# Layer norm, modulation, Hyena filters, long convolutions and the first head pair's projections written as one program block

## The reference, cut to what matters

```python
mod = (c @ w_ada + b_ada)[:, None, :]
shift, scale, gate = jnp.split(mod, 3, axis=-1)
h = (_layer_norm(x) * (1.0 + scale) + shift).astype(x.dtype)
p = h @ w_in + b_in
p_qkv, g_attn, p_hy, g_hy, r_merge = jnp.split(p, [i1, i2, i3, i4], axis=-1)
...
u = centred_conv3(p_hy, conv_w, conv_b)
v, x1, x2 = jnp.split(u, 3, axis=-1)
filters = implicit_filters(S, filt_w1, ...)     # 3 sine layers of width 64, then @ filt_w4, times a decay
z = v
for o, gate_o in enumerate((x1, x2)):
    z = gate_o * (bidirectional_long_conv(z, filters[:, o, 0], filters[:, o, 1]) + filt_bias[o] * z)
y_hy = z * jax.nn.silu(g_hy)
```

## Time and profile before

| what | value |
|---|---|
| median of 3 runs | 2665.92 us (2662.88 to 2666.19) |
| the profiled execution's own time | 2664.33 us |
| its span, first to last instruction | 2662.5 us |
| PE busy | 2415.2 us, 91% |
| DVE busy | 1003.7 us, 38% |
| ACT busy | 592.3 us, 22% |
| POOL busy | 243.0 us, 9% |
| mean granted PE clock | 0.937 |

### The profile page before, as it was taken

How to read it: one execution, slowest core, us unless ns; L and a number is a source line. 1 busy time by engine, 2 the same in 40 slices (tenths; PEclk the granted TensorE clock), 3 DMA queues, 4 the chain that set the end, 5 groups by cost and what they waited for, 6 DMA issues and landing times. The chain is left out here.

```text
span 2662.5 us, 23256 instructions
## 1 busy us (share of the span) xinstructions
PE 2415.2 (91%) x9479; PEld 1601.8 (60%) x9479; DVE 1003.7 (38%) x1690; ACT 592.3 (22%) x1010; POOL 243.0 (9%) x156
## 2 busy tenths in 40 slices
PE   6889998999958999999999999989598898998998
PEld 2433443444326777676776778866374675557975
DVE  3264441542442022322223222357766322344255
ACT  0210101001013233232332333101121343322032
POOL 0000000000002111111111112211000110000000
PEclk9788999999988999898998999999799899999999
DMA  7301022211203111111110121130410112003000
GB/s 278 96 27 44 20 83 77 78 51 59 63 24 103 48 33 32 39 34 32 37 36 25 41 83 44 44 140 31 138 16 4 40 40 91 1 1 127 36 36 40
DMA packets 131232, 151.18 MB, mean 57 GB/s; under 512 B 14501, under 2 KB 106115, under 8 KB 130309
## 3 DMA queue, kind: packets, MB, share of 16 engines
q1 hardware_dynamic: 119734, 107.82, 12.7%
q0 software_dynamic: 11392, 41.87, 4.7%
HBM read 136.89 MB, written 11.60 MB: 56 GB/s over the span
## 5 line engine op out<-in xcount | busy, mean ns | idle before, releaser
L168 PE MATMUL banks<-h_hi,da_w_rest 128*128 128x512 f32 x896 | 364.1, 406 | 40.5 <-DVE h_rest L1334 40.5
L169 PE MATMUL banks<-h_rest,da_w_hi 128*128 128x512 f32 x896 | 354.3, 395 | 0.0
L170 PE MATMUL banks<-h_hi,da_w_hi 128*128 128x512 f32 x896 | 353.0, 394 | 0.0
L434 PE MATMUL banks<-arena 128*128 128x512 f32 x512 | 242.0, 635 | 12.9 <-DMA arena<-in_w_in 12.9
L168 PEld LDWEIGHTS banks<-h_hi,da_w_rest 128*128 128x128 f32 x896 | 171.3, 191 | 96.8 <-issue 59.1
L584 PE MATMUL banks<-arena 128*128 128x512 f32 x480 | 209.9, 598 | 7.8 <-DMA arena<-in_fwd_C 3.7
L1005 POOL TENSOR_TENSOR da_w_rest<-arena,da_w_hi 128x1024 fp32r<-128x1024 f32 x56 | 134.5, 2402 | 712.2 <-ACT da_w_hi L1168 712.2
L434 PEld LDWEIGHTS banks<-arena 128*128 128x128 f32 x512 | 103.7, 205 | 154.8 <-issue 145.8
L1328 DVE COPY arena<-banks 128x768 f32<-128x768 f32 (+1 forms) x64 | 52.8, 825 | 378.9 <-PE banks L1081 378.9
L170 PEld LDWEIGHTS banks<-h_hi,da_w_hi 128*128 128x128 f32 x896 | 170.9, 191 | 37.6
L169 PEld LDWEIGHTS banks<-h_rest,da_w_hi 128*128 128x128 f32 x896 | 171.7, 192 | 33.3
(11 more groups left out here) (353 smaller groups left out, 3694.9 us busy)
## 6 DMA issues: line engine op xcount, KB each, us to landing
arena<-in_w_in SPq DMA_DIRECT2D x80, 512.0 KB, 3.8
arena<-in_w_ada POOLq DMA_DIRECT2D x6, 2048.0 KB, 10.5
arena<-in_decay SPq DMA_DIRECT2D x32, 256.0 KB, 2.9
arena<-in_x SPq DMA_DIRECT2D x4, 1024.0 KB, 15.2
arena<-in_fwd_P POOLq DMA_DIRECT2D x4, 1024.0 KB, 6.8
arena<-in_fwd_M POOLq DMA_DIRECT2D x4, 1024.0 KB, 8.3
arena<-in_fwd_B POOLq DMA_DIRECT2D x4, 1024.0 KB, 5.6
arena<-in_w_out SPq DMA_DIRECT2D x8, 512.0 KB, 7.6
```

The lines of the kernel that those rows point to most:

```text
L168: nc.tensor.matmul(out, ll, rh, start=start, stop=False)
L169: nc.tensor.matmul(out, lh, rl, start=False, stop=False)
L170: return nc.tensor.matmul(out, lh, rh, start=False, stop=stop)
L434: last = nc.tensor.matmul(PS[:, 2 * (n % 2) + h, :], self.wt[:, n % 4, k, :], self.hT[:, k, h * 512:(h + 1) * 512], start=(k == 0), stop=( ...
```

## The change

`prepare`, `hyena` and the start of `dilated_attention` become one block, `front`, with one hand-written order for each engine.

- The filter network works on both directions at once: 128 partitions by 1024 columns in place of 64 by 2048, so 6 products in place of 12. Filter rows take the two directions as two 64-row products side by side (partitions 0 to 63 and 64 to 127). The decay is computed by ACT as an exponential, no longer loaded. Filters come before the modulation; the spectra of order 1 are made first, written to DRAM and read back for order 1.
- Chunks 0 to 3 of the modulation use `c` itself as the stationary operand, one column wide (L441 of the changed kernel), and give one row; the two chunks of `gate` stay 128 columns wide.
- The transform has eight leaves of 128 complex points (N, C, B0, B1, P0, M0, P1, M1), 4 products each, in place of the five leaves with 60. An inverse takes 4 products a leaf as well. The leaves come out of DVE in three steps (`cyclic`, `cyclic_b`, `negacyclic_leaves`), and PE may start on a leaf once its step is done.
- The 16 Hyena projections are split products as well, in one stream of 26 tiles (`T_ALL`) with the 10 of head pair 0, over one weight ring. Leaves and inverses stand between tiles 4 and 5, 7 and 8, 11 and 12, and behind 12. The convolution adds its outer taps straight from PSUM.
- `dilated_attention` begins with the value rows; its first weights, tiles 10 and 11, and the distance table are loaded there.

The diff, cut to its core:

```diff
+            def filter_rows(stage, t):
...
+                bank_free(g, t)
+                for d in range(2):
+                    last = nc.tensor.matmul(PS[:, 4 + 2 * (t % 2) + d, :], h3[HD * d:HD * d + HD, t * P:(t + 1) * P], w4[HD * d:HD * d + HD, a, :],
+                                            start=True, stop=True)
+                last.then_inc(f_mm, 1)
...
+            def modulation(i):
...
+                for k in range(KT):
+                    if i < 2:
+                        last = nc.tensor.matmul(PS[:, 2 + i % 2, :], cbc[:, k, :], wada[:, i % 2, k, :], start=(k == 0), stop=(k == KT - 1))
+                    else:
+                        last = nc.tensor.matmul(PS[0:1, 2 + i % 2, :], cols2[:, 39 + k:40 + k], wada[:, i % 2, k, :], start=(k == 0), stop=(k == KT - 1))
+                last.then_inc(mod_done, 1)
...
+            def forward(g, l, base, first, ready, mm, loads):
+                done = groups[g][1]
+                pe.wait_ge(mat_in[l], 16 * loads)
+                pe.wait_ge(ready, done // 8 * 3 + LEAF_STEP[l])
+                bank_free(g, l)
+                ins = leaf_inputs(l, base, first)
+                for part in range(2):
+                    for k in range(2):
+                        last = nc.tensor.matmul(PS[:, 4 + 2 * (l % 2) + part, :], mats[:, l, k * 256 + part * P:k * 256 + part * P + P], ins[k],
+                                                start=(k == 0), stop=(k == 1))
+                last.then_inc(mm, 1)
...
+            def project(T):
+                pe.wait_ge(w_rest, T + 1)
+                if T >= 2:
+                    if T - 2 < X2:
+                        pe.wait_ge(row_ready, T - 1)
+                    elif T - 2 < GHY:
+                        pe.wait_ge(conv_done, T - 1)
+                    else:
+                        pe.wait_ge(p_ready, T - 1)
+                for h in range(2):
+                    for k in range(KT):
+                        if T == 0 and k % 2 == 0:
+                            pe.wait_ge(h_rest[h], k // 2 + 1)
+                        if h == 1 and k == 4 and 1 <= T <= X2:
+                            to_rows(T - 1)
+                        last = split_product(nc, PS[:, 2 * (T % 2) + h, :], tuple(v[:, k * P:(k + 1) * P] for v in w_parts[T % 2]),
+                                             tuple(v[:, k % 2, h * 512:(h + 1) * 512] for v in K.h_parts[k // 2]), k == 0, k == KT - 1)
+                    last.then_inc(proj_mm, 1)
+
...
+            for layer in range(3):
+                network(layer)
+            for t in range(NT):
+                filter_rows(0, t)
+            for i in range(3):
+                modulation(i)
+            for l in range(4):
+                forward(1, l, 3, 5, hl_ready, hs_mm, 1)
+            modulation(3)
+            for l in range(4, 8):
+                forward(1, l, 3, 5, hl_ready, hs_mm, 1)
+            modulation(4)
+            modulation(5)
...
+            for T in range(5):
+                project(T)
+            for l in range(8):
+                forward(3, l, 3, 5, hl_ready, hs_mm, 1)
+            for T in range(5, X2):
+                project(T)
+            for l in range(8):
+                forward(4, l, 6, 3, zl_ready, zs_mm, 1)
+            for l in range(8):
+                inverse(0, l)
+            for T in range(X2, GHY):
+                project(T)
+            for l in range(8):
+                forward(6, l, 6, 3, zl_ready, zs_mm, 3)
+            project(GHY)
+            for l in range(8):
+                inverse(1, l)
+            for T in range(GHY + 1, T_ALL):
+                project(T)
...
+            act.wait_ge(filt_in, 16 * 8)
+            decays(0, 0)
+            decays(0, 1)
+            act.wait_ge(nmr_ready, 1)
+            for t in range(2, NT):
+                decays(0, t)
+                normalise(t - 2)
...
+            def multiply(a, l):
...
+                dve.wait_ge(zs_mm, 8 * a + l + 1)
+                if a == 0 and l == 0:
+                    dve.wait_ge(hs_ready, 16)
+                if a == 1 and l % 4 == 0:
+                    dve.wait_ge(h1_in, 32)
+                nc.vector.tensor_tensor(t01, PS[:, b:b + 2, :], H, ALU.mult)
+                nc.vector.tensor_tensor(t23[:, 0, :], PS[:, b, :], hi, ALU.mult)
+                link(nc.vector.tensor_tensor(t23[:, 1, :], PS[:, b + 1, :], hr, ALU.mult), taken)
...
+                    link(nc.vector.tensor_tensor(hi, t23[:, 0, :], t23[:, 1, :], ALU.add))
+                    link(nc.vector.tensor_tensor(hr, t01[:, 0, :], t01[:, 1, :], ALU.subtract), products)
...
+            fold_filter(0)
...
+            total_and_difference(tile(4, 0, 4), tile(4, 4, 4))
+            cyclic(h_leaves)
+            cyclic_b(h_leaves)
+            negacyclic(3)
+            negacyclic_leaves(3, 5, h_leaves)
...
+            fold_filter(1)
...
+                nc.vector.tensor_tensor(lo[:, :, 0:512], hT[:, 2 * c:2 * c + 2, 0:512], hi[:, :, 0:512].bitcast(fp32), ALU.subtract).then_inc(h_rest[0], 1)
+            total_and_difference(tile(4, 0, 4), tile(4, 4, 4))
+            cyclic(h_leaves)
+            convolve(0)
+            cyclic_b(h_leaves)
+            negacyclic(3)
+            convolve(1)
+            negacyclic_leaves(3, 5, h_leaves)
+            for T in range(2, 5):
+                convolve(T)
+            dve.wait_ge(row_ready, 4)
+            dve.wait_ge(hs_mm, 16)
+            split_rows()
+            cyclic(z_leaves)
+            convolve(5)
+            cyclic_b(z_leaves)
+            negacyclic(6)
+            convolve(6)
+            negacyclic_leaves(6, 3, z_leaves)
+            convolve(7)
+            for l in range(8):
+                multiply(0, l)
+            recombine_cyclic(0)
+            convolve(8)
+            recombine_negacyclic(0)
+            convolve(9)
+            dve.wait_ge(row_ready, 8)
+            link(nc.vector.tensor_tensor(tile(6, 0, 8), tile(6, 0, 8), tile(5, 0, 8), ALU.mult), Count(z1_ready))
+            split_rows()
+            cyclic(z_leaves)
+            convolve(10)
+            cyclic_b(z_leaves)
+            negacyclic(6)
+            convolve(11)
+            negacyclic_leaves(6, 3, z_leaves)
+            for l in range(8):
+                multiply(1, l)
+            recombine_cyclic(1)
+            recombine_negacyclic(1)
...
-            for n in range(halves):
-                project(n)
...
-            round_weights(0)
-            for h in range(2):
-                for c in range(4):
-                    half = slice(h * 512, (h + 1) * 512)
-                    nc.scalar.copy(K.h_parts[c][0][:, :, half], hT[:, 2 * c:2 * c + 2, half]).then_inc(h_hi, 1)
-                if h == 0:
-                    round_weights(1)
-            act.wait_ge(yhy_out, 16)
-            for n in range(halves):
-                take_projection(n)
+            round_weights(TILES)
+            round_weights(TILES + 1)
+            act.wait_ge(K.yhy_out, 16)
```

More of the change, by code:

```diff
@@ L261, in _, with decays @@
         @block.scalar
         def _(act):
-            act.wait_ge(var_ready, 1)
-            nc.scalar.activation(std, mv[:, :, 1], ACT.Sqrt).then_inc(std_ready, 1)
+            def decays(stage, t):
+                n = 8 * stage + t
+                if n >= 2:
+                    act.wait_ge(f_ready, n - 1)
+                for d in range(2):
+                    last = nc.scalar.activation(dec[:, t % 2, d, :], delta, ACT.Exp, scale=tcol[:, 8 * d + t:8 * d + t + 1])
+                last.then_inc(dec_ready, 1)
@@ new lines, in _ @@
+            for layer in range(3):
+                act.wait_ge(fn_arg, layer + 1)
+                nc.scalar.activation(h3 if layer == 2 else hA, hA, ACT.Sin).then_inc(fn_sin, 1)
+            act.wait_ge(var, 1)
+            nc.scalar.activation(rstd, mv[:, :, 1], ACT.Sqrt).then_inc(std, 1)
+            act.wait_ge(filt_in, 16 * 8)
[5 more added lines that the diff above has]
+                normalise(t - 2)
@@ new lines, in negacyclic_leaves @@
+            def negacyclic_leaves(v, first, signal):
+                x0, x1, y0 = two((v, 0), (v, 2)), two((v, 4), (v, 6)), two((v, 1), (v, 7))
+                for x, l0, cy0, cy1 in ((x0, 0, C8, -S8), (x1, 2, S8, C8)):
+                    axpy(both(first, l0), y0, cy0, x)
+                    axpy(tile(first, l0), tile(v, 5), cy1, tile(first, l0))
+                    axpy(tile(first, l0 + 1), tile(v, 3), cy1, tile(first, l0 + 1))
+                    axpy(x, x, 2.0, both(first, l0), ALU.subtract, signal if l0 else None)
@@ L290, in _ @@
+            statistics(0)
+            statistics(1)
+            network(1)
+            for i in range(2, 6):
+                statistics(i)
+            network(2)
+            statistics(6)
+            statistics(7)
             for i in range(NT):
                 link(nc.vector.bn_aggr(mv[:, i, :], stats[:, i, :]))
-            link(nc.vector.tensor_scalar(mv[:, :, 1], mv[:, :, 1], 1e-5, None, ALU.add), Count(var_ready))
```

(7 more changed lines are left out.)

1067 lines of the change are left out of this document (504 added, 563 removed).

## The result

The changed kernel takes 2434.19 us (median of 4 runs, 2432.76 to 2436.55), the kernel before beside it 2666.06 us: ratio 0.913, 95% interval 0.912 to 0.915. That is 231.9 us less. The forecast was 2417, so it was 17 us too low: 1 us above the forecast's own range (2402 to 2433) and inside the whole range (2400 to 2460).

The account below looks back on a forecast made before the run. The first 922 us were taken as bound by PE, with holes at the start and of 39 us. Gain 251 less 3 for hand-overs, 248, from 2664.3 gives 2416; with 1.6 to the median, 2417; range 2400 to 2460.

Parts of the forecast that it names:

- (a): Start of the front block: 26 small loads put the first PE instruction at 16 us, bounds 9.7 and 24.
- (b): Filter network: three layers take 36.5 us, to 52.5; aggregation and ACT's table loads follow, to 60.3.
- (d): PE-bound modulation chunks 41.2 us, eight leaves 27.4, one-column products 4.6, clock ramp 2, wait 1.6: ends at 151.
- (e): Filling hT until 173 us, then PE waits for DVE's fold, 9.6, and first piece of h_rest, 1.7: 184.4.
- (g): DVE starts the spectrum products at 312 us, 4.1 a leaf; the inverse runs behind and ends at 369.
- (h): Tiles 8 to 11: convolution 8 ahead of recombine_negacyclic, convolution 9 at 407.7 us; PE waits 5, to 418.6.
- (i): DVE's gate, split, leaf steps and convolutions from 407.7 to 444.5 us; PE idles some 20; last leaf ends at 472.
- (k): Tiles 13 to 25 take 141.7 us, to 652.5; each needs its weights within 10.9.
- (l): End of front: eviction and barrier 2.7 us, distance table issue 2, landing 11.3, scaling 2; first value copy at 671.
- rival 1: Modulation: the clock falls in the four one-column chunks, +28 us, 2445; chance 27%.
- Rival 2: DVE comes too late for the transposes if PSUM or strided-pair passes are 15% longer: +45 us, 2462; chance 15%.
- The sum of 189 us: PE work saved in the front: projections 45 us, forward products 96, inverses 43, filter network 5.

Follow-up runs that it names:

- the fold behind the split: Changed kernel with the second filter's fold on VectorE behind the four subtractions of h instead of ahead of them: 2432.73 us.
- the five moves: Changed kernel with table early, convolution 8 behind recombination, tile 12 in the hole, h's rest on VectorE ahead of the fold, convolution 0 right behind it: 2402.60 us.
- two rests sooner: Against the kernel that makes weight rests of tiles 0 to 12 on VectorE, not GpSimd: those of tiles 2 and 3 moved forward; 2389.38 us.

## Why the prediction was right, and where not

The walk against the traces, in us; the last column is the run in which GpSimd only fills:

| point | walk | changed kernel | with the fill |
|---|---|---|---|
| first PE instruction (a) | 16 | 14.1 | 14.8 |
| first filter row (b) | 60.3 | 56.2 | - |
| transposes into hT begin (d) | 151 | 152.0 | - |
| tile 0 begins (e) | 184.4 | 188.4 | 188.2 |
| spectrum products begin (g) | 312 | 332.2 | 320.9 |
| convolution 9 ends (h) | 407.7 | 432.0 | 414.5 |
| third leaf's product begins on DVE (i) | 444.5 | 471.2 | 451.7 |
| last tile ends (k) | 652.5 | 677.5 | 658.6 |
| first value copy (l) | 671 | 691.3 | 672.6 |

In row (i) the walk's figure is the end of DVE's leaf step and the trace's the first product behind it.

- (a) to (d), right within about 4 us, in part by luck. The first filter row came 4 us sooner than walked, but from it to the last one PE took 19.0 us, not 13.7; the two errors cancel at (d). At the granted clock of 0.50 a pair of filter rows took 1.9 us (two in 3.78), where the prediction weighed 1.7 and 2.5. The four one-column chunks were the largest doubt (rival 1, 27%). They kept the full clock; windows over the first one and the last two:

```profile
91.10:98.00 6.90, 6.90 (x16) 1.22 (x16) 6.73 (x6) 0.00 (x0) 0.00 (x0) 1.00 0.85 302
...
132.90:146.70 13.80, 13.80 (x33) 2.54 (x32) 0.00 (x0) 1.59 (x2) 0.56 (x1) 1.00 0.36 152
```

  Each took 6.9 us, as the forecast had it, and as the rule that the prediction took from the Trainium skill (page "TensorE: Matmul & The Clock Gate", section "What's actually happening") would have it. Rival 1 is refuted.
- (e) to (i) are the steps that failed. The prediction priced each DVE pass by its own duration and POOL's rest only as a link in the chain of weights (k). The missing term is their mutual hold-up: 4 us at the start of tile 0 (the fold's second pass takes 6.5 us, not 4.4, and the first piece of `h_rest` 3.4, not 1.7; PE waited 16.4 us there, not 10 to 12), and nine times 2.1 behind it. With the subtractions gone the walk's waits (h) and (i) come out within half a us, and the front ends 18.7 us sooner.
- What is then left of the walk is 4 us at the start of tile 0 and 6 to 9 in all from (g) to the last tile. PE's clock behind each wait is part of the rest (0.50 from 188.4 to 192.5 us, 0.61 from 432 to 438); it was argued from such windows and not tested.
- (l) was 5 too long: from the last tile's end to the first value copy are 13.8 us, against 18.5. The table is the wait, as its move showed, but it landed 7.2 us after its issue (median of the two halves), not 11.3. That took 5 us off the miss at the end, which is luck as well:

```profile
689.19 2.09 DVE L1396 TENSOR_SCALAR arena<-arena 128x1536 f32<-128x1536 f32 x2 [115.00 <-DMA arena<-in_dist]
```

- Rival 2 (15%) named the right place and the wrong cause. DVE did come late for the transposes and for the chain of (h) and (i). But passes that read PSUM or strided pairs cost what rows 6 say (1.23 and 0.68 us in the spectrum products), and its price of 45 was twice the loss. The measured time lies above the forecast's own range and is inside the whole one only by the room left for rivals 1 and 2, neither of which is what happened.
- PE's busy time was put at 2225 and is 2174. The sum of 189 us took full-clock prices; the 512 records of the old projections show 242 us, not 219, and the filter rows, of which the sum says nothing, fell from 42 to 22. The walk did not use that sum, so the time is not touched by it; what falls is the prediction's account of how much of the gain is PE work.

The sum then: the last tile ended 25 us later than walked, (l) gave 5 of them back, so the first value copy came 20 us late, and the prediction had set 3 us aside for hand-overs; that leaves the 17. (The prediction's own terms add up to 2417.7, which it wrote as 2417.) With the subtractions of tiles 2 to 15 replaced by fills, 18.7 of the 20 are gone.

## What to carry to other kernels

Where a walk rests on a chain of VectorE passes with two SBUF inputs, look at what GpSimd does in the same microseconds: its two-operand passes are not free, even at 11% busy, and may be cheaper on VectorE itself. Where one engine's work fills the gap, ask what the next step waits for before you put that work in another order: in three runs here (the fold behind the split, the five moves, two rests sooner) the wait came back one step on, under another name or behind another tile. Waits that the walk shows to stand alone (a load behind a barrier, a tile that fits a hole) are worth their length; by the traces these three added up (31.1 us one by one, 31.9 in the kernel with two moves more).

## What the runs showed of the hardware

- A two-operand subtraction over 1024 columns on GpSimd (2.39 us alone) and a VectorE pass with two SBUF operands do not overlap: whichever comes second takes about its own time and the rest of the other's (VectorE 0.69 to 2.86 and 2.29 to 4.37 us; GpSimd 2.39 to 3.40 at 403.64 us of the changed kernel). Even a pass over two columns took 1.21 us, not 0.16. VectorE passes with one operand in PSUM are not held: with the five moves, two convolution taps took 2.60 us, as always, while a subtraction of 2.36 us ran from their middle on.

```profile
410.39 2.60 DVE L699 SCALAR_TENSOR_TENSOR arena<-banks,arena 128x1023 f32<-128x1023 f32 x2
411.85 2.36 POOL L395 TENSOR_TENSOR fr_w_rest<-arena,fr_w_hi 128x1024 fp32r<-128x1024 f32 x1 [8.01 <-ACT fr_w_hi L577]
413.02 1.21 DVE L760 TENSOR_TENSOR arena<-arena 128x2 f32<-128x2 f32 x1
```

- A fill over 1024 columns on GpSimd (0.95 us) held nothing up: passes of 0.69 and 2.29 us beside it kept their length.
- GpSimd pays as well: its four pieces of h took 4.1 us each beside VectorE's.
- One-column matmuls of 512 columns, back to back, kept the full clock (1.00 over 13.8 us), where the 4-row and 64-row stretches of the earlier trace rows show 0.74 and 0.50. Why these differ was not tested.
